# A two-block transformer kernel: weight buffers and weight ring at byte 32 of a 64-byte line, token buffers at byte 0

## What is computed

```python
h = h + parallel_mixer(rms_norm(h, norm_mix_g), w_in, ...)
h = h + memory_cross_attention(rms_norm(h, norm_xattn_g), rms_norm(mem, norm_mem_g), ...)
u = jax.nn.relu(rms_norm(h, norm_mlp_g) @ mlp_w1)
h = h + (u * u) @ mlp_w2
...
x = x + 0.5 * swiglu(rmsnorm(x, ffn1_norm), w1, w3, w2)
x = x + token_mix(rmsnorm(x, mix_norm), w_in, ...)
x = x + 0.5 * swiglu(rmsnorm(x, ffn2_norm), w1, w3, w2)
return rmsnorm(x, final_norm)
```

## Time and profile before

| | |
|---|---|
| median of 3 runs | 2128.43 us (2128.05 to 2129.41) |
| span of the profiled execution, first to last instruction | 2126.9 us |
| PE busy | 2109.0 us, 99% |
| PEld busy | 1825.0 us, 86% |
| DVE busy | 1399.3 us, 66% |
| ACT busy | 1053.6 us, 50% |
| granted TensorE clock | 1.000 on average, so 2.4 GHz |

### The profile page before, as it was taken

One profiled execution on the slowest core, in us unless ns is written; L12 is line 12 of the kernel. 1 busy time (PEld: TensorE's weight loads), 2 busy tenths in 40 slices (PEclk: granted clock), 3 DMA queues, 4 the chain that ended last, 5 costly groups with the idle time before them and its releaser, 6 DMA issues.

```text
span 2126.9 us, 33395 instructions
## 1 busy us (share of the span) xinstructions
PE 2109.0 (99%) x13388; PEld 1825.0 (86%) x13388; DVE 1399.3 (66%) x2337; ACT 1053.6 (50%) x1766; POOL 51.9 (2%) x68
## 2 busy tenths in 40 slices
PE   9999999999999999999999999999999999999999
PEld 7888988888988988899988878887777888899997
DVE  4664664467765767788856677746776357678874
ACT  6664545443533543464543466545667234345454
POOL 0000000000000011110100000000000000000000
PEclk9999999999999999999999999999999999999999
DMA  5221522147364366875543622321010332345422
GB/s 190 60 80 61 179 99 75 45 137 199 94 175 124 112 161 159 228 203 164 149 139 91 189 81 84 100 84 49 28 51 25 95 99 90 110 123 156 129 90 79
DMA packets 212875, 243.83 MB, mean 115 GB/s; under 512 B 9953, under 2 KB 197490, under 8 KB 212210
## 3 DMA queue, kind: packets, MB, share of 16 engines
q1 hardware_dynamic: 201458, 208.15, 31.1%
q0 software_dynamic: 11264, 33.56, 7.3%
HBM read 232.77 MB, written 35.65 MB: 126 GB/s over the span
## 4 chain that ended last, share of the span: by engine, by line
PE 94%; DVE 3%; ACT 1%; issue 1%; DMA 1%; SPq 0%; DVEq 0%; ACTq 0%
PE lin L968 19%; PE lin L970 18%; PE lin L969 18%; PE turned L1069 3%; PE score L1164 3%; PE score L1529 3%; PE score L1530 3%; PE mix L1529 3%; PE mix L1530 3%; PE score L1528 3%; PE mix L1528 3%; PE mix L1178 2%; PE turned L1529 1%; PE turned L1530 1%; PE turned L1528 1%
## 5 line engine op out<-in xcount | busy, mean ns | idle before, releaser
L968 PE MATMUL lin<-xh,wh 128*128 128x512 f32 (+1 forms) x968 | 382.6, 395 | 2.1 <-DVE wl L2789 1.4
L970 PE MATMUL lin<-xh,wl 128*128 128x512 f32 (+1 forms) x968 | 369.9, 382 | 0.0
L969 PE MATMUL lin<-xl,wh 128*128 128x512 f32 (+1 forms) x968 | 368.9, 381 | 0.0
L968 PE MATMUL lin<-ah,wh 128*128 128x512 f32 x724 | 283.6, 392 | 1.4 <-DVE al L2794 0.6
L970 PE MATMUL lin<-ah,wl 128*128 128x512 f32 x724 | 281.1, 388 | 0.0
L969 PE MATMUL lin<-al,wh 128*128 128x512 f32 x724 | 281.0, 388 | 0.0
L2783 DVE TENSOR_TENSOR wl<-raw,wh 128x2048 fp32r<-128x2048 f32 x77 | 176.5, 2292 | 118.9 <-ACT wh L1868 118.9
L968 PEld LDWEIGHTS lin<-xh,wh 128*128 128x128 f32 x968 | 182.2, 188 | 43.3 <-issue 9.6
L970 PEld LDWEIGHTS lin<-xh,wl 128*128 128x128 f32 x968 | 182.0, 188 | 36.6
L969 PEld LDWEIGHTS lin<-xl,wh 128*128 128x128 f32 x968 | 182.5, 188 | 32.5 <-issue 1.0
L1868 ACT ACTIVATE wh<-raw 128x2048 fp32r<-128x2048 f32 x77 | 146.7, 1906 | 87.9 <-PE lin L970 76.3
(11 more groups left out here) (563 smaller groups left out, 4775.7 us busy)
## 6 DMA issues: line engine op xcount, KB each, us to landing
raw<-in_w_in_dram SPq DMA_DIRECT2D x38, 1024.0 KB, 5.3
raw<-in_ffn_w_dram SPq DMA_DIRECT2D x46, 512.0 KB, 4.6
raw<-in_mlp_w_dram SPq DMA_DIRECT2D x20, 1024.0 KB, 5.5
raw<-in_ffn_w_dram SPq DMA_DIRECT2D x20, 1024.0 KB, 5.4
up_sums_ffn<-in_ffn_w_dram POOLq DMA_DIRECT2D x32, 512.0 KB, 5.5
down_sums_ffn<-in_ffn_w_dram POOLq DMA_DIRECT2D x24, 512.0 KB, 5.9
raw<-in_xattn_wkv_dram SPq DMA_DIRECT2D x8, 1024.0 KB, 5.3
raw<-in_w_out_dram SPq DMA_DIRECT2D x8, 1024.0 KB, 5.2
```

Source lines behind the costliest of these rows:

```text
L968: nc.tensor.matmul(o, w[0], x[0], start=first, stop=False)
L969: nc.tensor.matmul(o, w[0], x[1], start=False, stop=False)
L970: return nc.tensor.matmul(o, w[1], x[0], start=False, stop=last)
```

## The change

Four things get other addresses, and nothing else changes: the instructions of every engine, their order, sizes and waits stay as they are. A buffer of 64 bytes behind xh and one of 32 bytes before wh shift what follows; the ring slot in the arena begins 8 floats later, the token sums 16 floats later, and the two weight slots in xh begin 32 bytes later than xh itself.

```diff
+HALF_LINE = 32
...
         xh = sb("xh", [PART, KT, T], F32R)
         xh_f = nc.alloc_sbuf_tensor_at("xh_f", [PART, 4, HT, PC], F32, offset=xh_at)
+        sb("after_xh", [PART, 16])
+        xh_blocks = nc.alloc_sbuf_tensor_at("xh_blocks", [PART, 4, HT, PC], F32R, offset=xh_at + HALF_LINE)
...
         raw = sb("raw", [PART, 2, KT, PC])
+        sb("before_wh", [PART, HALF_LINE // 4])
         wh = sb("wh", [PART, 2, KT, PC], F32R)
...
-        A = Arena(N_end)
-        XS_h, XS_l = (Arena(N_end + e * 7 * HT * PC, arena_r)(7 * HT, PC).rearrange("p (b k) n -> p b k n", b=7) for e in range(2))
-        A = Arena(N_end + 2 * 7 * HT * PC)
+        xs_at = N_end + HALF_LINE // 2
+        XS_h, XS_l = (Arena(xs_at + e * 7 * HT * PC, arena_r)(7 * HT, PC).rearrange("p (b k) n -> p b k n", b=7) for e in range(2))
+        A = Arena(xs_at + 2 * 7 * HT * PC)
...
-        RING_h, RING_l = (Arena(e * HT * PC, arena_r)(HT, PC) for e in range(2))
+        RING_h, RING_l = (Arena(HALF_LINE // 4 + e * HT * PC, arena_r)(HT, PC) for e in range(2))
...
-            x = xh.rearrange("p k n -> p (k n)").rearrange("p (b k n) -> p b k n", b=4, k=HT)
-            return x[:, 2 * (slot - 4)], x[:, 2 * (slot - 4) + 1]
+            return xh_blocks[:, 2 * (slot - 4)], xh_blocks[:, 2 * (slot - 4) + 1]
```

## The result

| | before | after |
|---|---|---|
| median, 4 runs each | 2128.55 us (2128.05 to 2129.41) | 2152.37 us (2152.20 to 2152.55) |
| span of the profiled execution | 2126.9 us | 2150.4 us |
| ratio of the runs | | 1.0112, 95% interval 1.0099 to 1.0124 |

The change makes the kernel 1.1% slower. The prediction was 2113 us with 0.47 on faster; its sign is wrong, and the measured time lies above its range of 2092 to 2150 us.

What follows compares the result with a forecast made beforehand. PE bounds the kernel, busy 2109.0 of 2126.9 us, so matmul steps set the time. Terms -2.4 + 4.7 - 1.3 - 16.8 = -15.8 us give 2111.1, plus 1.5 for the median 2112.6, forecast 2113 us, range 2092 to 2150.

Steps and rivals of the forecast that it cites:

- linears, 4812 x -3.5 ns: 4812 512-column linear matmuls, whose weights move to byte 32 of a 64-byte line, each step 3.5 ns cheaper: -16.8 us.
- weights moving, 960 x -2.5: 960 matmuls with weights as moving operand, going from same half to halves apart, 2.5 ns cheaper each: -2.4 us.
- token sums with wh, wl or a slot: 3168 matmuls with token sums moving lose the good combination, 1.5 ns dearer each: +4.7 us; surest in sign.
- ring, hidden values and tokens at 256 columns: 528 token sums with the ring, 792 hidden values with wh, wl: same half to apart, -1 ns each, -1.3 us.
- The same 32-byte half costs most, whichever half it is.: At 256 columns, both operands in the same half of a 64-byte line cost most: records 283 ns against 280 to 282.
- The four combinations of the earlier trace: 256-column products, moving / stationary byte modulo 64: 0 / 0 and 0 / 32 at 0.1200 us, 32 / 0 at 0.1175.
- From 256 to 512 columns: Gain for the 512-column linears extended from the 256-column pair's 2.5 ns, 4812 x -2.5 = -12.0 us, taken a little further.
- 7 ns can be had: Linears could gain 7 ns each, as a plain fp32 matmul's record is 382 ns against 389: -33.7 us.
- The rival at 0.38: Linears lose their even beat, +3.3 ns a step, +15.9 us; all parts +21.4 us, 2150 us; chance 0.38.
- That nothing else moves: DVE, ACT and DMA: shifted writes cost nothing, 0 us; no instruction, order or wait changes, only steps can.
- The rival at 0.15: Whole kernel: linears independent of the half, or their gain pays for token sums; 2126 to 2132 us, named 2128; chance 0.15.
- the one at 0.12: Collisions vanish: linears fall to the plain fp32 matmul's level, -33.7 us; in all -39.4 us, 2089 us; chance 0.12.

Runs made afterwards that it cites:

- map_distances: PE alone, whole model left out: 24 settings of 96 matmuls at 512 and 256 columns, operand distances 0 to 224 bytes in steps of 32; 436.74 us.
- all_pad32: Kernel before plus a 32-byte buffer before xh, so later buffers shift together and all product distances stay; 2128.36 us, ratio 0.9998 to before.
- weights_pad64: Kernel before plus only a 64-byte buffer before wh; 2146.98 us, ratio 1.0083 to before.
- weights_pad32: Kernel before plus only a 32-byte buffer before wh; 2147.47 us, ratio 1.0087 to before.
- sums64: Kernel before with token sums 288 bytes later and the ring 96 bytes later, so all products with token sums have distance 64; 2122.07 us, ratio 0.9968.
- map_entries: PE alone, model left out: 16 settings (512 and 256 columns, distances 0 to 224), each entered after seven different short preludes of matmuls; 1247.65 us.
- change_but_weights: Changed kernel without the 32 bytes before wh, 256 bytes behind xh for 64, weight slots still 224 from the sums; 2127.82 us, ratio 0.9995 to before.

## Why the prediction was wrong

| term | predicted, us | measured, us |
|---|---|---|
| linears, 4812 x -3.5 ns | -16.8 | +27.8 |
| weights moving, 960 x -2.5 | -2.4 | +0.2 |
| token sums with wh, wl or a slot | +4.7 | +1.2 |
| ring, hidden values and tokens at 256 columns | -1.3 | -2.5 |
| everything else | 0 | -3.0 |
| sum | -15.8 | +23.7 |

**The step that failed is the term of the linears**, "I take -3.5 ns, a little beyond the 256-column pair, since the load is less pressed". It measured +6.3 ns (ah, al) and +5.8 ns (xh, xl), and +26 to +28 us in place of -16.8. It had three supports, and each gave way.

- *"The same 32-byte half costs most, whichever half it is."* The four combinations of the earlier trace rows were read modulo 64. By distance they are four points of another table: 0 / 0 and 32 / 32 are distance 0, 32 / 0 is 96, 0 / 32 is 160. The rows fitted both readings, and "0 / 32" of before says nothing about "0 / 32" of after, which is distance 32. map_distances, all_pad32 and weights_pad64 decide between them.
- *From 256 to 512 columns.* In map_distances distance 0 is 1.7 ns dearer than 32 at 256 columns and 6.7 ns cheaper at 512. A gain read at one length had the wrong sign at the other.
- *"7 ns can be had"*, from the plain fp32 row L1451. It kept its 382 ns, but no fp32r setting at 512 columns went under 226.7 ns from any of the eight distances or seven entries. That row is of another type and gives no floor for this one.

**The rival at 0.38 had the mechanism**, that the even beat belongs to distance 0 and is lost, and missed in the size. Its +3.3 ns came from ten steps after a wait. Those average the way into the good beat at distance 0, not the settled beat of another distance; that is 6.7 ns dearer at distance 32. So its +15.9 us should have been up to 4812 x 6.7 = +32 us; the mean over the kernel is 5.8 to 6.3 ns, since part of the linears of before had not settled at 226.7 either (228.2 on average for xh and xl). Its smaller terms were high in turn (+7.9 for the sums, measured +1.2), and its total of 2150 us lies near the 2152.4 measured in part because these errors cancel, which is luck.

**Weights moving** was the term with the longest row, and it failed as well: the change doesn't bring the 32 / 0 of the earlier trace rows (distance 96) but 160 for two of the three matmuls of a triple and 224 for one. At 160 alone the map has 120.0; in weights_pad32, at 224 for all three, these products do fall to 117.0. **Token sums** rose, the step called surest, by +0.7 ns with wh, wl for the 1.5 taken; those with a slot fell.

**That nothing else moves** held for DVE, ACT and the DMAs. Only the last row of the account, -2.8 us, was not foreseen: the chain has 96% PE and 2% DVE where it had 94% and 3%, which fits PE waiting a little less when it is itself slower. It was not tested by itself.

A rule that the prediction set aside: the runs show steps from 226.7 to 234.2 ns for the same 512-column fp32r matmuls, by the distance of two addresses alone and with PE alone on the core. The Trainium skill (TensorE: Matmul & The Clock Gate, in its section Step-by-step: what each phase is for, on loading the stationary operand) says that the load has a read port of its own and takes no bandwidth from the running matmul; by that rule the change would cost nothing, and the trace disagrees by 23.5 us. The rival at 0.15, nothing measurable, fails by the same number; the one at 0.12, a fall to the level of the fp32 row, fails with the third support.

What stays open: why the period is 256 bytes, why a distance has the beat that it has, and why at 256 columns one distance keeps either of two beats. The runs show the table, and that the same matmuls at the same addresses keep one beat or the other after different work; what chooses, and what happens inside PE or SBUF, is not shown. Of the period, the runs show that a shift of 256 bytes gives the steps of 0, and that no shift of 32 to 224 does at 512 columns.

## What to carry to other kernels

Where fp32r matmuls and weight loads follow each other without a gap, read the step from the timeline and compute, for each kind of product, the distance between the stationary and the moving operand modulo 256 bytes: here offsets alone cost up to 1.1% and gave 0.6% without moving an instruction, and 32 bytes in front of one buffer cost 0.9%. Measure the distances at the length that the kernel uses, since here the best distance at 512 columns was among the dearest at 256, and keep the largest class at its best distance first. A pattern in the rows of the old kernel that fits a rule at one period should be tried against other periods before it is extended to a combination that the kernel does not hold.

## What the runs showed of the hardware

- The steady step of a 512-column fp32r matmul with a 128-column load each, over multiples of 32 bytes, is 226.7 ns at distance 0 (and at 256), 228.9 at 192 and 232.4 to 234.2 at the six others. At the granted clock of 1.00 (2.4 GHz) 226.7 ns are 544 cycles, 512 + 32, and 233.3 ns are 560, 512 + 48.
- At 256 columns the steps are 113.3 to 120.0 ns; 113.3 ns, 272 cycles or 256 + 16, is reached at distances 64 and 192 alone, and only from some entries. It lasts: 196 rows in sums64, 48 (all that there were) in map_entries. Distance 192 shows it in a whole kernel too: hidden values with the ring step at 113.3 ns in change_but_weights.
- Where the pair of operands lies doesn't matter: with both 32 bytes later, 226.7 and 120.0 ns again, and the kernel at 0.9998 of its time.
- A triple with mixed distances has a step of its own: 234.8 to 235.4 ns with 96, 32, 96 in the changed kernel, where 96 alone takes 234.2 and 32 alone 233.3.
